# Gate columns carried in a first value slab, row maxima sent through GpSimd's queue, and one residual ahead of a weight split

## What is computed

```
h = rms_norm(x, g[0])
q, k, v, o, gates = split(h @ w_in)          # gates: 8 columns, 4 input and 4 forget gates
gates = 15 * tanh((gates + b_gates) / 15)
ig, logf = gates[:4], log_sigmoid(gates[4:])
bcum = cumsum(logf)                           # over the tokens
m_t = max(running max over s <= t of (ig - bcum), 0) + bcum
scores = (q k^T) * exp(bcum_t - bcum_s + ig_s - m_t)      # causal
...
x = x + cross_attn(rmsnorm(x), mem_n)         # its last product is with xa_wo
x = x + conv_glu_ffn(rmsnorm(x), ...)         # its first product is with ffn_w_up
```

## Time and profile before

| | |
|---|---|
| median of 3 runs | 945.97 us (945.75 to 946.73) |
| the profiled execution | 945.98 us, span in the trace 943.8 us |
| busy: PE, DVE, ACT, POOL | 99%, 68%, 57%, 11% |
| mean granted PE clock | 0.997 of full |

### The profile page before, as it was taken

One profiled execution on the slowest core, in us unless ns is written; L12 is line 12 of the kernel. 1 busy time (PEld: TensorE's weight loads), 2 busy tenths in 40 slices (PEclk: granted clock), 3 DMA queues, 4 the chain that ended last, 5 costly groups with the idle time before them and its releaser, 6 DMA issues.

```text
span 943.8 us, 19963 instructions
## 1 busy us (share of the span) xinstructions
PE 934.4 (99%) x8026; PEld 929.0 (98%) x8026; DVE 646.2 (68%) x888; ACT 536.0 (57%) x759; POOL 100.8 (11%) x96
## 2 busy tenths in 40 slices
PE   9999999999999999999999999999999999999997
PEld 9999999999999999999999999999999999999997
DVE  6768687665445886688665444894775689999652
ACT  6666657664444555556665444565554567676442
POOL 0210200000000000109100000006030120000001
PEclk9999999999999999999999999999999999999998
DMA  8653546556545465455546555544353255555531
GB/s 331 253 178 120 197 155 223 199 181 212 187 178 194 157 223 186 178 180 184 218 178 209 193 183 202 185 182 176 133 180 134 93 182 217 182 204 193 206 107 45
DMA packets 26855, 172.72 MB, mean 183 GB/s; under 512 B 3492, under 2 KB 4136, under 8 KB 6568
## 3 DMA queue, kind: packets, MB, share of 16 engines
q1 hardware_dynamic: 26504, 171.30, 50.9%
q10 hardware_dynamic: 288, 0.52, 0.2%
HBM read 170.76 MB, written 1.05 MB: 182 GB/s over the span
## 4 chain that ended last, share of the span: by engine, by line
PE 94%; DVE 2%; issue 1%; ACT 1%; DMA 1%; POOL 0%; POOLq 0%; SPq 0%; ACTq 0%
PE po L469 26%; PE po L471 26%; PE po L470 26%; PE po L496 2%; PE po L497 2%; PE po L498 2%; PE third L469 2%; PE third L470 2%; PE third L471 2%; DVE wL L1390 1%; PE pc L819 1%; ACT wH L901 1%; DMA raw<-in_weights 1%; PE pn L566 1%; PE pn L556 0%
## 5 line engine op out<-in xcount | busy, mean ns | idle before, releaser
L1390 DVE TENSOR_TENSOR wL<-raw,wH 128x1024 fp32r<-128x1024 f32 x314 | 382.9, 1241 | 162.3 <-ACT wH L901 162.2
L901 ACT ACTIVATE wH<-raw 128x1024 fp32r<-128x1024 f32 x314 | 329.1, 1057 | 231.4 <-PE po L471 217.5
L469 PE MATMUL po<-xnH,wH 128*128 128x256 f32 x1280 | 359.2, 281 | 2.1 <-DVE xnL L1397 1.0
L470 PE MATMUL po<-xnL,wH 128*128 128x256 f32 x1280 | 354.5, 277 | 0.0
L471 PE MATMUL po<-xnH,wL 128*128 128x256 f32 x1280 | 354.5, 277 | 0.0
L469 PEld LDWEIGHTS po<-xnH,wH 128*128 128x128 f32 x1280 | 240.7, 188 | 3.6 <-issue 1.8
L470 PEld LDWEIGHTS po<-xnL,wH 128*128 128x128 f32 x1280 | 240.7, 188 | 0.3
L471 PEld LDWEIGHTS po<-xnH,wL 128*128 128x128 f32 x1280 | 240.6, 188 | 0.0
L471 PE MATMUL po<-hH,wL 128*128 128x256 f32 x688 | 189.9, 276 | 0.0
L469 PE MATMUL po<-hH,wH 128*128 128x256 f32 x688 | 189.9, 276 | 0.0
L470 PE MATMUL po<-hL,wH 128*128 128x256 f32 x688 | 189.9, 276 | 0.0
(11 more groups left out here) (313 smaller groups left out, 1187.1 us busy)
## 6 DMA issues: line engine op xcount, KB each, us to landing
raw<-in_weights SPq DMA_DIRECT2D x157, 1024.0 KB, 4.8
raw<-in_weights SPq DMA_DIRECT2D x8, 256.0 KB, 5.6
mem<-in_memT SPq DMA_DIRECT2D x1, 1024.0 KB, 12.3
out<-y SPq DMA_DIRECT2D x4, 256.0 KB, 2.6
x<-in_xT ACTq DMA_DIRECT2D x2, 256.0 KB, 4.2
x<-in_xT SPq DMA_DIRECT2D x2, 256.0 KB, 6.5
rows<-maxima SPq DMA_DIRECT2D x1, 512.0 KB, 3.5
decayt<-in_decay SPq DMA_DIRECT2D x1, 512.0 KB, 6.0
```

Of the source, the lines that this page charges most:

```text
L469: pe.matmul(psum[:, n, 0:T], wH[w][:, wc], aH[:, ac, :], start=start, stop=False)
L470: pe.matmul(psum[:, n, 0:T], wH[w][:, wc], aL[:, ac, :], start=False, stop=False)
L901: act.activation(wH[b % HL][:, hs], raw[b % RAW][:, hs], ACT.Copy).then_inc(s_hi, 1)
L1390: dve.tensor_tensor(wL[b % HL][:, hs], raw[b % RAW][:, hs], wH[b % HL][:, hs].bitcast(f32), ALU.subtract)\
```

## The change

The first slab is now the first value slab, of group `v0`, multiplied by token. Its halves lie in new buffers `vH` and `vL`, whose rows have 256 value columns and, behind them, the 8 gate columns, split in two like any weight; so each of its 48 matmuls has 264 columns. The 16 matmuls of `gates` are gone, and `gz` is read from the value group. The gate weights are loaded on ACT's queue ahead of the second piece of `x`, and ACT and DVE split them in the first quarter. The four `qk` slabs follow as slabs 1 to 4, then three `v` slabs.

`log_sums` moves to chunk 2 of the third slab of `qk` (counted from 0: slab `qk` 2), `turn_a` to chunk 5 of it, the first scores to chunk 2 of the next value slab. On DVE, `log_sums`' readers and the running maxima move ahead of splits, keeps and memory pairs. The two transfers of the maxima leave SP's queue and go to POOL's, ahead of its additions of squares. Before `fup`, the last residual and feed move ahead of the first half of a split.

```
-    ("qk", 4, 4, "V"), ("v", 4, 4, "A"), ("o", 4, 4, "V"),
+    ("v0", 1, 1, "A"), ("qk", 4, 4, "V"), ("v", 3, 3, "A"), ("o", 4, 4, "V"),
...
+        vH = sb("vH", [P, C, 3 * P], f32r, at)
+        vL = sb("vL", [P, C, 3 * P], f32r, at)
...
 SP
-            sp.wait_ge(s_mrow, 1)
-            sp.dma_start(maxima, mrow[0][:, P:P + T]).then_inc(s_out_rows, 16)
-            sp.wait_ge(s_out_rows, 16)
-            sp.dma_start(rows[:, :, :], maxima.partition_broadcast(P)).then_inc(s_rows, 16)
...
 PE
+                        if (j, k) == (0, 0):
+                            pe.wait_ge(s_wgL, 1)
                         for n in range(2):
-                            mm = products(slot(j), n, j, k, xnH, xnL, k, k == 0, k == 7)
+                            if j == 0:
+                                tc = slice(n * P, n * P + P)
+                                both = slot(0)[:, n, 0:VD + 2 * NH]
+                                pe.matmul(both, xnH[:, k, tc], vH[:, k, 0:VD + 2 * NH], start=k == 0, stop=False)
+                                pe.matmul(both, xnL[:, k, tc], vH[:, k, 0:VD + 2 * NH], start=False, stop=False)
+                                mm = pe.matmul(both, xnH[:, k, tc], vL[:, k, 0:VD + 2 * NH], start=False, stop=k == 7)
+                            else:
+                                mm = products(slot(1), n, 1, k, xnH, xnL, k, k == 0, k == 7)
...
-            first_slabs({6: lambda: gates(0, range(4)), 7: lambda: gates(0, range(4, 8))})
-            phase_slab("qk", 2, xnH, xnL, between={0: lambda: norm_sums(0), 2: lambda: gates(1, range(4)), 3: lambda: norm_spread(0), 5: lambda: gates(1, range(4, 8))})
-            phase_slab("qk", 3, xnH, xnL, between={6: log_sums})
-            phase_slab("v", 0, xnH, xnL, by_token=True, between={1: turn_a})
-            phase_slab("v", 1, xnH, xnL, by_token=True, between={2: first_scores, 3: turn_maxima, 7: lambda: scores(1)})
-            phase_slab("v", 2, xnH, xnL, by_token=True, between={4: lambda: scores(2)})
-            phase_slab("v", 3, xnH, xnL, by_token=True, between={1: lambda: scores(3)})
+            first_slabs()
+            phase_slab("qk", 1, xnH, xnL, between={0: lambda: norm_sums(0), 3: lambda: norm_spread(0)})
+            phase_slab("qk", 2, xnH, xnL, between={2: log_sums, 5: turn_a})
+            phase_slab("qk", 3, xnH, xnL)
+            phase_slab("v", 0, xnH, xnL, by_token=True, between={2: first_scores, 3: turn_maxima, 7: lambda: scores(1)})
+            phase_slab("v", 1, xnH, xnL, by_token=True, between={4: lambda: scores(2)})
+            phase_slab("v", 2, xnH, xnL, by_token=True, between={1: lambda: scores(3)})
...
 DVE, before fup
-            for i in range(2, 4):
-                split(o0 + i + 2, halves=(0,))
-                residual("wo", i)
-                feed_pair(6, i, "gffn")
-                split(o0 + i + 2, halves=(1,))
+            split(o0 + 4, halves=(0,))
+            residual("wo", 2)
+            feed_pair(6, 2, "gffn")
+            split(o0 + 4, halves=(1,))
+            residual("wo", 3)
+            feed_pair(6, 3, "gffn")
+            split(o0 + 5)
...
 POOL
             factor(0)
+
+            pool.wait_ge(s_mrow, 1)
+            pool.dma_start(maxima, mrow[0][:, P:P + T]).then_inc(s_out_rows, 16)
+            pool.wait_ge(s_out_rows, 16)
+            pool.dma_start(rows[:, :, :], maxima.partition_broadcast(P)).then_inc(s_rows, 16)
             norm(1)
```

More of the change, by code:

```diff
@@ L59, in source @@
 def source(s):
+    if s == 0:
+        return 4
     if s == SLAB0["f7"]:
         return SLAB0["wo"] - 1
-    return s - 1 if SLAB0["f7"] < s < SLAB0["wo"] else s
+    return s - 1 if s <= 4 or SLAB0["f7"] < s < SLAB0["wo"] else s
 PCOL, _c = {}, 0
@@ L329, in build @@
         in_third = [GROUP0[name] for name in ("f0", "f1", "f2", "f3")]
-        in_third += [GROUP0[name] + 2 for name in ("qk", "up0", "cin", "up1", "rq", "wo", "fup")]
+        in_third += [GROUP0[name] + 2 for name in ("v0", "up0", "cin", "up1", "rq", "wo", "fup")]
         def place_of(g):
@@ L394, in _ @@
             stop = SLAB0["rq"] // RAW + 1
-            for s in range(RAW, 10):
+            sp.wait_ge(s_lo, 2)
+            sp.dma_start(raw[0][:, :], weights[source(4), :, :]).then_inc(s_raw[0], 16)
+            for s in range(RAW + 1, 10):
                 load(s, s % RAW)
-            sp.wait_ge(s_mrow, 1)
-            sp.dma_start(maxima, mrow[0][:, P:P + T]).then_inc(s_out_rows, 16)
-            sp.wait_ge(s_out_rows, 16)
-            sp.dma_start(rows[:, :, :], maxima.partition_broadcast(P)).then_inc(s_rows, 16)
             for s in range(10, 12):
@@ L611, in turn_head @@
                 mm.then_inc(s_hT, 1)
[L613 to L620, removed]
             def log_sums():
@@ L907, in split_quarter @@
                     act.wait_ge(loaded[q], 16)
-                    k = act.activation(wH[b][:, qs], raw[b][:, qs], ACT.Copy)
+                    src = raw[b][:, qs]
+                    if b == 0:
+                        k = act.activation(vH[:, 2 * q:2 * q + 2, 0:VD], src.rearrange("p (k n) -> p k n", k=2), ACT.Copy)
+                    else:
+                        k = act.activation(wH[1][:, qs], src, ACT.Copy)
                     if q < 3:
@@ L981, in _ @@
                 feed_hi(q, "g00", (s_x[q], 16))
+                if q == 0:
+                    act.wait_ge(s_wg, 16)
+                    act.activation(vH[:, :, VD:VD + 2 * NH], wg[:, :, :], ACT.Copy).then_inc(s_wgH, 1)
                 split_quarter(q)
@@ L997, in _, with keep_vx @@
             act.activation(softp[:, :, :], fexp[:, :, :], ACT.Ln, bias=1.0).then_inc(s_sp, 1)
+            v0 = SLAB0["v"] - 1
+            def keep_vx(h):
+                keep_values("v" if h else "v0", max(h - 1, 0), lambda t: vx[:, t, h, 0:VD], rtok, 1)
+            keep_vx(0)
             split(4)
+            act.wait_ge(s_par, 16)
+            mem_pair(0)
+            split(5)
             mem_pair(1)
-            split(5)
-            v0 = SLAB0["v"]
-            def keep_vx(h):
-                keep_values("v", h, lambda t: vx[:, t, h, 0:VD], rtok, 1)
             def decays(h):
@@ L1465, in _ @@
                         k.then_inc(s_lo, 2)
[L1466 to L1469 removed]
             sum_squares(0)
[L1471 removed]
+            split(2)
             mean_square(0)
[L1473 to L1474 removed]
+            split(3, halves=(0,))
+            dve.wait_ge(s_par, 16)
+            dve.wait_ge(s_r, 1)
+            psum = group("v0", 0)
+            for t in range(TT):
+                k = dve.scalar_tensor_tensor(gz[:, t, :], psum[:, t, VD:VD + 2 * NH], rtok[:, t:t + 1], col("bgates", 0, 2 * NH),
+                                             ALU.mult, ALU.add)
+            k.then_inc(s_gz, 1)
+            split(3, halves=(1,))
             dve.wait_ge(s_Rs, 1)
             keep("qk", 0, qT[:, 0:2, :])
[L1477 to L1483 removed]
             dve.wait_ge(s_gt, 1)
             dve.tensor_scalar(gcap[:, :, :], gt[:, :, :], CAP, None, ALU.mult).then_inc(s_gcap, 1)
[L1486 to L1488 removed]
+            keep("qk", 1, qT[:, 2:4, :])
             dve.wait_ge(s_cum, 1)
@@ L1493, in _ @@
             dve.tensor_tensor(av[:, :, :], gcap[:, :, 0:NH], sums, ALU.add).then_inc(s_av, 1)
-            keep("qk", 3, kT[:, 2:4, :])
-            split(5)
+            split(4)
             dve.wait_ge(s_avT, 1)
@@ L1507, in _ @@
             assert a == 0
+            keep("qk", 2, kT[:, 0:2, :])
+            split(5)
+            mem_pair(0)
             mem_pair(1)
+            keep("qk", 3, kT[:, 2:4, :])
             def exponents(h):
```

59 lines of the change are left out of this document (23 added, 36 removed).

## The result

| | before | after |
|---|---|---|
| median | 945.97 us | 941.7 us (9 runs, 940.77 to 944.74) |
| the profiled execution, its span | 945.98, 943.8 | 941.22, 939.4 |

The account below looks back on a forecast made before the run. PE, busy for 99% of the span, was taken to bound the kernel. 945.98 - 2.65 (first stage) + 1.3 (one addition) - 1.0 (step into `fup`) = 943.6 us; range 941.8 to 946.3.

Parts of the forecast that it names:

- What gets in: I take one: 1.3 us back: First stage: one POOL addition of squares gets among DVE's split and memory pairs, delaying the first scores by 1.3 us.
- When POOL is free: First stage: POOL, done with its two transfers of the maxima, can start its additions of squares at about 38.6.
- two ends: Bounds for POOL being free: 37.0 if transfers go as SP's did, 40.1 if held until `rows` has landed.
- POOL comes too late to harm: Rival, first stage: POOL free after 39.1, no addition delays DVE, the 2.65 us stay won: 942.3; chance 0.26.
- more additions: Rival, first stage: two additions get in, 944.9, chance 0.20; three or four, 945.6 to 946.3, 0.13 at full clock.
- the Trainium skill's 2.0 us for each transfer: Estimate for transfers issued from GpSimd: with SP's 0.35 of issue, POOL free at 37.4, three or four additions, about 946.
- The first stage: Up to the first scores: they start 2.65 us earlier, before 1.3 us is given back for one addition.
- The step into `fup`: First `fup` slab: PE's 1.14 us wait for DVE's `xnL` goes, 0.2 back for pace; gain 1.0 (0.5 to 1.15).
- The sum: Whole kernel: 945.98 - 2.65 + 1.3 - 1.0 = 943.6 us.
- The range's low end: Whole kernel: 941.8 us, with no addition and the bounds of the start and the pace in its favour.

Follow-up runs that it names:

- second profiled execution: Profile of the changed kernel run once more with no edit; that run's median was 941.98 us.

## Why the prediction was wrong, step by step

**The step that failed** is "What gets in: I take one: 1.3 us back". When POOL is free came out right, 38.59 for 38.6, in part by luck: 38.6 was the middle of two ends, from the maxima to a free POOL it took 3.0 us and not 3.6, and the maxima came 0.56 late. The rule was not right: that an addition coming in the midst of DVE's operations gets in after the next one. It was read from places where DVE itself had a gap (753.57 to 753.82) or was met by an addition already running (746.71). Neither says what happens to an addition that meets a chain without a gap, and that one waits until the chain has a gap or comes to an operation that reads PSUM: 2.55 us, 2.58, 4.47 and 3.34 in four kernels, with every DVE operation ahead of that point at its own length. The 1.3 are 0. Where an addition comes first, the rule does hold (3.2 us at the scores with the transfers on SP's queue).

The rival with the nearest time, "POOL comes too late to harm" (942.3), had the time by a wrong way: POOL was not late. The two estimates that rested on POOL being freed sooner, "more additions" and the Trainium skill's 2.0 us for each transfer (DMA: Bandwidth & Descriptors, "Anatomy of one DMA — SWDGE (gpsimd) path"), did not come about either: POOL was free at 38.59, not at 37.0 to 37.4. From the first issue to the second it took 2.14 us, which agrees with that page; but POOL's queue was not held by the second for longer than its record of 0.58, since the addition began at 38.6 and lasted 1.30 where DVE left the way free.

**The first stage** was mis-sized a little: 2.25 at the first scores, forecast 2.65. The second `qk` slab began at 19.59 (19.3), the log sums at 28.38 (27.9 to 28.2) without a wait, as forecast, and the rest of the chain followed. PE waited 0.3 us for the last keep (up to 0.6).

**The step into `fup`**: 1.0 forecast, for a PE at the slower pace. At that pace it is 1.07, at the faster 1.76, and the order alone gives 1.1 us in the median; undone in the changed kernel it costs about 2 (943.85 against 941.7 and 941.98, in other batches). In the profiled executions the pace happened to change as well: 1.31 from the first `fup` matmul on, and 0.65 ahead of it.

**The sum.** With 0 for the additions, 2.14 for the first stage and 1.07 for `fup` the forecast would have been 942.8. The 0.3 us outside the span, which the prediction took as unchanged, make it 942.4: that is the second profiled execution, 942.4, with the slower pace at the `wo` slabs. With the chance of the pace it is 941.8 (first profiled execution 941.22; medians 941.7 and 941.98). The range's low end allowed for no addition and for a start and a pace there in its favour, but not for the 0.3 us outside the span nor for the pace of 154 matmuls elsewhere; either is more than the 0.1 us by which it was missed.

## What to carry to other kernels

Before pricing what DVE and GpSimd take from each other, ask who comes first. In these traces a queue of DVE operations with two inputs in SBUF and without a gap loses nothing to a GpSimd addition that arrives in its midst, while one addition that is there ahead of it lets the next ones in too (0 against 3.2 us). So a transfer put ahead of GpSimd's work can be worth more as a delay than as a transfer. And when an engine waits, what it wins by coming sooner counts only with the wait taken away: the same order was worth 1.07 us at one pace and 1.76 at the other.

## What was not expected of the hardware

One program runs at two paces of its matmuls at the same granted clock, 0.113 and 0.1175 us. In these traces the pace can change where the row of matmuls is interrupted, if only by some 0.01 us, and stays until the next interruption. Between two profiles of the changed kernel it changed for a stretch of 154 matmuls (0.65 us) and for four others of 77 to 173, some to the faster and some to the slower pace; and in one execution of the kernel with only the new `fup` order for a stretch of 1408 (6.0 us). The stretch of 1408 followed a wait of 0.08 us for a PSUM group; other stretches behind a longer wait, like that ahead of `fup`, went at the faster pace. So what chooses the pace stays open, and that a time 6 us above the rest comes from such a stretch was seen in one trace alone.

PE's wait of 3.4 us in the first stage took the granted clock to 0.50 for some 3 us, 1.5 us of further loss, while the wait of 1.6 us ahead of `fup` left it at 1.00.
